# Semaphores in two sets cleared inside the next stage, and the experts' gathered rows in a ring of four

## The reference

```python
mod = jax.nn.silu(c) @ p["w_ada"] + p["b_ada"]          # shifts, scales and gates of both halves
h = rmsnorm(x, p["norm_mix_g"]) * (1.0 + sc1) + sh1
proj = h @ p["w_in"]
qa, fa, ia, ga, bb, cc, vb, mga, mgb = jnp.split(proj, _split_points(), axis=-1)
ya, s_hgrn_new = hgrn2_branch(qa, fa, ia, ga, s_hgrn, lb, p["hgrn_norm_g"])     # gated linear recurrence
yb, s_conv_new = short_conv_branch(bb, cc, vb, s_conv, p["conv_w"], p["conv_b"])
mixed = (jax.nn.sigmoid(mga) * (ya @ p["w_out_hgrn"])
         + jax.nn.sigmoid(mgb) * (yb @ p["w_out_conv"]))
x = x + g1 * (mixed @ p["w_o"])
h2 = (rmsnorm(x, p["norm_ffn_g"]) * (1.0 + sc2) + sh2).reshape(B * T, D)
top_i, top_w = route(h2, p["w_router"], p["router_bias"])      # 8 of 64 experts, from 4 of 8 groups
ffn = (routed_experts(h2, top_i, top_w, p["w_exp_gate"], p["w_exp_up"], p["w_exp_down"])
       + swiglu(h2, p["w_sh_gate"], p["w_sh_up"], p["w_sh_down"]))
x = x + g2 * ffn.reshape(B, T, D)
```

## Time and profile before

| | us |
|---|---|
| median of 3 runs (lowest, highest) | 2221.73 (2220.11, 2222.01) |
| the profiled execution's own time | 2220.11 |
| its span, first to last instruction | 2218.5 |
| TensorE busy, whole span | 1982.7 (89%) |
| expert stage, 1171.3 to 2167.7 | 996.4, TensorE busy 941.9 |
| final stage, 2169.1 to 2218.5 | 49.4, TensorE idle |

### The profile page before, as it was taken

The page is one execution under the profiler, slowest core; times in us unless marked ns, Lnnn a source line. Parts: engine busy times, 40 slices in busy tenths (PEclk is TensorE's granted clock), DMA queues, the critical chain, the costliest instruction groups (busy, mean ns, idle before and its releaser), DMA issues. The chain is left out here.

```text
span 2218.5 us, 32929 instructions
## 1 busy us (share of the span) xinstructions
PE 1982.7 (89%) x9599; PEld 1472.1 (66%) x9601; DVE 1037.9 (47%) x1508; ACT 889.3 (40%) x1213; POOL 346.4 (16%) x321
## 2 busy tenths in 40 slices
PE   4799999799989899797887999999999999999970
PEld 3799999576656566584545767666666776776650
DVE  3210111533327433443625666655555666666656
ACT  4111110234301221211135666656565666666652
POOL 0100100100000000000102222222222232322320
PEclk9899999899989999898988999999999999999995
DMA  6211110111132466334128999999999789879846
GB/s 230 68 47 39 55 40 19 42 42 51 41 92 86 150 220 237 136 135 167 64 94 345 310 299 290 349 340 343 375 343 368 248 264 284 263 237 307 277 98 248
DMA packets 152434, 424.08 MB, mean 191 GB/s; under 512 B 11455, under 2 KB 76211, under 8 KB 127810
## 3 DMA queue, kind: packets, MB, share of 16 engines
q1 hardware_dynamic: 118258, 298.98, 35.8%
q0 software_dynamic: 31488, 114.93, 20.1%
q10 hardware_dynamic: 2640, 9.54, 1.1%
HBM read 345.93 MB, written 77.49 MB: 191 GB/s over the span
## 5 line engine op out<-in xcount | busy, mean ns | idle before, releaser
L1915 DVE TENSOR_TENSOR wexp_lo<-wexp,wexp_hi 128x2048 fp32r<-128x2048 f32 x190 | 426.9, 2289 | 45.8 <-ACT wexp_hi L1867 42.0
L1867 ACT ACTIVATE wexp_hi<-wexp 128x2048 fp32r x190 | 352.8, 1904 | 51.9 <-issue 49.3
L1848 PE MATMUL bank<-wexp_down,hTe 128*128 x736 | 330.6, 592 | 0.0
L1823 PE MATMUL bank<-wexp_hi,x_hi 128*128 128x512 f32 x744 | 300.2, 403 | 4.0 <-DVE wexp_lo L1915 4.0
L1823 PE MATMUL bank<-wexp_hi,x_lo 128*128 128x512 f32 x744 | 291.9, 392 | 0.0
L1823 PE MATMUL bank<-wexp_lo,x_hi 128*128 128x512 f32 x744 | 290.6, 391 | 0.0
L1797 POOL DMA_INDIRECT acc_d<-ob,ixs x92 | 160.0, 1739 | 654.1 <-DMA acc_d<-ob,ixs 280.9
L556 PE MATMUL bank<-hT,wg 128*128 128x344 f32 x768 | 238.0, 464 | 21.1 <-DMA wg<-in_w_in 14.9
L1848 PEld LDWEIGHTS bank<-wexp_down,hTe 128*128 128x128 f32 x736 | 139.1, 189 | 139.4 <-issue 132.3
L556 PEld LDWEIGHTS bank<-hT,wg 128*128 128x128 f32 x768 | 145.2, 194 | 109.6 <-ACT gst L567 15.9
L458 PE MATMUL bank<-hT_hi,w_hi 128*128 128x344 f32 x576 | 186.7, 324 | 14.8 <-DVE w_lo L525 14.8
(11 more groups left out here) (320 smaller groups left out, 2693.5 us busy)
## 6 DMA issues: line engine op xcount, KB each, us to landing
wexp<-in_w_exp_gate SPq DMA_DIRECT2D x64, 1024.0 KB, 7.4
wexp<-in_w_exp_up SPq DMA_DIRECT2D x64, 1024.0 KB, 11.8
wexp_down<-in_w_exp_down SPq DMA_DIRECT2D x64, 1024.0 KB, 11.3
wada<-in_w_ada SPq DMA_DIRECT2D x12, 2048.0 KB, 11.1
w_raw<-in_w_in SPq DMA_DIRECT2D x28, 512.0 KB, 3.9
gates_d<-gst POOLq DMA_DIRECT2D x48, 172.0 KB, 2.1
gate<-gates_d SPq DMA_DIRECT2D x16, 516.0 KB, 5.5
wg<-in_w_in SPq DMA_DIRECT2D x16, 512.0 KB, 4.2
```

The costliest lines, as they stand in the source:

```text
L1823: last = pe.matmul(banks[0][:].rearrange("p (g n) -> p g n", g=2), stat[:, b, k, :], mov[:, b, :, k * FF:(k + 1) * FF], start=(k == 0 and ...
L1848: last = pe.matmul(banks[4 + half][:], hT[:, f, :], wdn[:, bass.ds(slot, 1), f, half * 512:half * 512 + 512].rearrange("p a n -> p (a n)") ...
L1867: act.activation(w_hi[:, b, g, :], wexp[:, bass.ds(e & (RING - 1), 1), g, :].rearrange("p a n -> p (a n)"), ACT.Copy).then_inc(whi_ok, 1)
L1915: dve.tensor_tensor(w_lo[:, b, g, :], wexp[:, bass.ds(e & (RING - 1), 1), g, :].rearrange("p a n -> p (a n)"), w_hi[:, b, g, :], ALU.subtr ...
```

## The change

Two things, in one edit.

Semaphores come from two sets in turn. `next_stage()` no longer opens a block; it gives the names of the set before last free and remembers the last stage's semaphores in `past`. The clears, `tidy(pool)`, stand in POOL's list of the next stage. The last stage has none, so the 20 semaphores of `experts` are not cleared any more.

In the expert stage `xg`, `ix` and `gat` have four buffers, and a block is gathered six blocks ahead of the one that is scattered (AHEAD, 4 before), so POOL's gather in `block_of(i)` is for block i+6 and its buffer is that of block i+2. Blocks 2 and 3 are gathered at once when the stage begins. To make room, `par` and `cT` are placed where they end with the trunk, and the tile of zeros for the pads is 256 instead of 512 wide, read twice by its DMA. DVE waits for the pads before its loop.

```diff
-AHEAD = 4
+AHEAD = 6
...
-        stage = top.enter_context(ExitStack())
-        held = []
+        stages = [top.enter_context(ExitStack()), top.enter_context(ExitStack())]
+        held, past = [], []
...
         def next_stage():
 
-            with nc.Block() as block:
-                @block.gpsimd
-                def _(pool):
-                    for s in held:
-                        pool.sem_clear(s)
+            stages[1].close()
+            stages.reverse()
+            past[:] = held
             held.clear()
-            stage.close()
+
+        def tidy(pool):
+
+            for s in past:
+                pool.sem_clear(s)
...
         @block.gpsimd
         def _(pool):
+            tidy(pool)
 
             with pool.Fori(0, PASSES) as i:
...
                 pool.memset(vblk[:], 0.0).then_inc(const_ok, 1)
+                tidy(pool)
                 pool.sem_inc(gate_read, 1)
...
                 pool.memset(badd[:], 0.0).then_inc(zero_ok, 1)
+                tidy(pool)
...
                     pool.dma_start(xt[0:rows_of(t), t % 2, :], x_rows(t)).then_inc(x_in[t % 2], 16)
+                    if t == 1:
+                        tidy(pool)
...
+                tidy(pool)
                 for r, (f, n) in enumerate(pieces):
...
-            xg = nc.alloc_sbuf_tensor_at("xg", [P, 2, XW], F32, offset=at)
+            xg = nc.alloc_sbuf_tensor_at("xg", [P, RING, XW], F32, offset=at)
...
         def gathered(i, q, ahead):
 
-            return (i - q) * 8 + 16 * ((q + ahead) // 2 + 1)
+            return (i - q) * 4 + 16 * ((q + ahead) // RING + 1)
...
             @block.gpsimd
             def _(pool):
+                for q in range(2, RING):
+                    pool.indirect_dma_start(out=xg[:, q, 0:XW], out_offset=None, in_=xe_d,
+                                            in_offset=bass.IndirectOffsetOnAxis(ap=ix[q][:, 0:1], axis=0)).then_inc(gat[q], 16)
                 pool.memset(none[:], 0.0).then_inc(pad_ok, 1)
...
-                def gather(j, b):
-                    pool.wait_ge(ix_ok, j - 1)
+                tidy(pool)
+
+                def gather(j, q):
+                    pool.wait_ge(ix_ok, j - (RING - 1))
...
-                for j in range(2, 4):
-                    pool.wait_ge(x_tp, j - 1)
-                    pool.wait_ge(wc_ok, j - 1)
-                    gather(j, j % 2)
+                for j in range(RING, AHEAD):
+                    pool.wait_ge(x_tp, j - (RING - 1))
+                    pool.wait_ge(wc_ok, j - (RING - 1))
+                    gather(j, j % RING)
 
                 def block_of(i, q):
                     b = q % 2
                     pool.wait_ge(x_tp, i + 3)
                     pool.wait_ge(wc_ok, i + 3)
-                    gather(i + 4, b)
+                    gather(i + AHEAD, (q + AHEAD) % RING)
                     pool.wait_ge(ob_ok, 2 * i + 4)
...
                 def block_of(i, q):
                     b = q % 2
                     take(i + 2, b)
-                    to_gather(i + 4, b)
+                    to_gather(i + AHEAD, (q + AHEAD) % RING)
...
+                dve.wait_ge(added, 32)
                 blocks(dve, block_of)
```

More of the change, by code:

```diff
@@ L399, in layer @@
             lists = far("lists", [P, ITEMS + AHEAD], U32)
-            ix = [far(f"ix{b}", [P, 1], U32) for b in range(2)]
-            xg = nc.alloc_sbuf_tensor_at("xg", [P, 2, XW], F32, offset=at)
+            ix = [far(f"ix{b}", [P, 1], U32) for b in range(RING)]
+            xg = nc.alloc_sbuf_tensor_at("xg", [P, RING, XW], F32, offset=at)
             next_stage()
@@ L405, in layer @@
             down_in = top.enter_context(nc.semaphore("down_in"))
-            gat = [top.enter_context(nc.semaphore(f"gat{b}")) for b in range(2)]
-            routing(nc, a, sb, sem, banks, ident, hT, xe_d, acc_d, table, starts, total, lists, ix, xg, gat, wexp, wdn,
+            gat = [top.enter_context(nc.semaphore(f"gat{b}")) for b in range(RING)]
+            routing(nc, tidy, a, sb, sem, banks, ident, hT, xe_d, acc_d, table, starts, total, lists, ix, xg, gat, wexp, wdn,
                     up_in, down_in)
@@ L410, in layer @@
             next_stage()
-            experts(nc, a, sb, sem, banks, ident, xe_d, acc_d, table, starts, total, lists, ix, xg, gat, wexp, wdn, up_in,
+            experts(nc, tidy, a, sb, sem, banks, ident, xe_d, acc_d, table, starts, total, lists, ix, xg, gat, wexp, wdn, up_in,
                     down_in)
@@ L1661, in _ @@
                 s.link(dve.tensor_tensor(lists[:, 0:ITEMS], ids[:, 0, :], ids[:, 1, :], ALU.add))
-                for b in range(2):
+                for b in range(RING):
                     dve.tensor_copy(ix[b][:], lists[:, b:b + 1]).then_inc(ix_ok, 1)
@@ L1802, in _, with turn @@
                 pool.wait_ge(added, 16 * n + 32)
-                for b in range(2):
-                    pool.wait_ge(gat[b], 16 * ((n + 5 - b) // 2))
+                for q in range(RING):
+                    pool.wait_ge(gat[q], 16 * ((n + AHEAD + RING - 1 - q) // RING))
             @block.tensor
             def _(pe):
-                def turn(j, b, here):
-                    pe.wait_ge(gat[b], here)
+                def turn(j, q, here):
+                    pe.wait_ge(gat[q], here)
                     if j is not 0:
@@ L1813, in turn @@
                     for k in range(KD):
-                        last = pe.transpose(banks[1 + k // 4][:, (k % 4) * P:(k % 4 + 1) * P], xg[:, b, k * P:(k + 1) * P],
+                        last = pe.transpose(banks[1 + k // 4][:, (k % 4) * P:(k % 4 + 1) * P], xg[:, q, k * P:(k + 1) * P],
                                             ident[:])
@@ L1839, in block_of @@
                     last.then_inc(h_tp, 1)
-                    turn(i + 2, b, gathered(i, q, 2))
+                    turn(i + 2, (q + 2) % RING, gathered(i, q, 2))
                     up(i + 1, 1 - b)
@@ L1931, in _ @@
                 take(0, 0)
-                to_gather(2, 0)
+                to_gather(4, 0)
                 rest_of_weights(e, 0, 0)
@@ L1940, in _ @@
                 e = entry(dve, 2, 1, E - 1)
-                weight(e, 2, 32)
+                weight(e, 2, 16)
                 rest_of_weights(e, 2, 0)
```

49 lines of the change are left out of this document (25 added, 24 removed).

## The result

The changed kernel takes 2195.89 us (median of 4 runs, 2195.29 to 2197.40) against 2221.87 us before (4 runs, 2220.11 to 2222.97): a ratio of 0.9887, 95% interval 0.9873 to 0.9901. That is 26.0 us less. The forecast was 2193 us in 2174 to 2210. On another chip, later, the same pair gave 2196.04 and 2221.13 us, ratio 0.9886 (0.9870 to 0.9901). The profiled execution took 2195.8 us (2220.11 before), its span is 2194.0 us. The profiled execution before was the shortest of its four, so the two spans differ by 24.5 us where the medians differ by 26.0.

The account below looks back on a forecast made before the run. It took expert-stage scatters, each waiting for the last one's landing, to bound the kernel, TensorE's pace hardly shorter. 13.4 + 15 = 28.4 us off 2220.1 gave 2191.7; with the median 1.6 us higher, 2193, range 2174 to 2210.

Parts of the forecast that it names:

- The clearing blocks: Seven blocks between stages that only clear semaphores: 177 clears and seven barriers leave the path, 13.4 us, bounds 11.5 to 14.5.
- The start of the expert stage: Two gathers moved to the front and DVE's new wait for the pads: 0 to 4 us, value 0.
- The ring: Four gather buffers in the expert stage: of 35.6 us TensorE loses, 19.2 stay; gain 16.4, valued at 15 us.
- the chain: Expert-stage scatters, each waiting for the one before to land: 948.3 us, 29 of it air; it stays after the change.
- The lag it allows: How late a scatter may be before TensorE loses time: 5.9 us before, 12.7 after, 6.8 gained once per slow stretch.
- the long stretch: 30 scatters from 1399.75 to 1716.31: 316.6 us against TensorE's 290.6; of 26.0 too much, 6.8 absorbed, 19.2 stay.
- The 1.4 us for longer landings: Allowance for scatter landings growing 0.05 us over 29 links, as the same bytes must move in less time.
- What was to show it: Signs named beforehand, including 70 or more scatters 0.8 us after a landing and TensorE's expert-stage loss near 20 us.
- A: Rival: in the expert stage scatters land faster and all 35.6 us come back; 49 us gained, 2173 us; 17%.
- B: Rival: full DMA engines hold TensorE to their pace, the expert stage gains nothing; 13.4 us gained, 2208 us; 17%.
- C: Rival: expert-stage scatters land later as weight loads overlap them more often; 2252 us at 0.8 us more per landing; 7%.
- D: Rival: the clears do not leave the path, because a POOL queue is waited for; 15 us gained only, 2207 us; 4%.

Follow-up runs that it names:

- e1_clears: The kernel before with only the clears moved into the next stage on POOL, the ring of gathered rows left two deep: 2204.82 us, ratio 0.9927.
- e5_thin: The changed kernel with only an eighth of each weight transfer of experts 4 and up: 2174.73 us, ratio 0.9788.
- e3_two: The changed kernel with scatters going to two accumulators in turn, the second added in the last stage by accumulating transfers: 2189.88 us, ratio 0.9861.
- e7_extra: The changed kernel with one more 0.52 MB transfer per block on POOL's queue: 2237.12 us, ratio 1.0070.

## Why the prediction was right

**The clearing blocks: 13.4 us forecast, 13.8 measured.** The clears' spacing and the seven barriers gave it. That POOL's work in the stages behind hides them holds too: in e1_clears no stage that took clears in is more than 0.2 us longer. In the mixers the first gate product starts at 411.39 us, when its weights land, where it was 412.55.

**The start of the expert stage: 0 forecast.** From the release to the third turn it took 19.3 us, 20.0 before. Nothing came back here.

**The ring: 15 us forecast, 13.1 measured (35.6 to 22.5).** The mechanism was right in each part. The named wait went, the chain stayed (316.56 and 316.72 us for the same 30 scatters), and the next limit is the landing that the index copy waits for. The lag it allows was forecast as 5.9 and 12.7 us; measured plateaus are 7.9 and 15.3. The sums took turns 10.02 us apart, but at the plateau TensorE goes at the chain's 10.92 us: two such intervals make the first 7.7, three make the second 15.4. The difference, which is what counts, is 7.4 against 6.8.

The term mis-sized is how much of this lag the long stretch gets. I gave it all 6.8 us. But the deeper ring also lets the lag of the blocks ahead be carried in: the first scatter of the stretch stands 1388.98 - 1379.80 = 9.2 us behind its turn (5.9 before), the last one 15.0. So 5.8 us were absorbed and TensorE lost 310.9 - 290.6 = 20.3 us over these turns, not 19.2, and another 2.2 us in the two intervals behind, while the lag ran off. That is 22.5. The 1.4 us for longer landings was an error: landings did not grow, the stretch is unchanged to 0.2 us. That it brought the value from 16.4 to 15, nearer to the 13.1 measured, is luck. All of the loss lies between the turns at 1430 and 1713 us.

Where the 13.1 us came from is worth seeing. Over the long stretch and the two intervals behind it the kernel before lost 25.0 us, so the deeper ring saved 2.5 there. The other 10.6 us were lost outside of it, in short runs of slow scatters, and there all of it came back.

**The sum.** 13.8 + 12.3 us in place of 13.4 + 15, and about 1.5 us given back by the other stages. Such shifts show between all of these programs (see the first turns in the table) and have no term in the prediction; they are within its range.

**What was to show it.** No clears between two barriers, no gather ahead of TensorE's transposes, 81 scatters (70 or more were named) released by a landing, the loss ahead of the hh transposes and inside the long stretch: all as written. The mean landing could not be read, since the trace of the changed kernel doesn't pair its scatters with their landings; that the same 30 scatters take the same time stands for it. The whole chain gives a bound, as an estimate: 935.2 us for 91 intervals, less the 0.8 us between a landing and the next start, is at most 9.5 us for the mean landing, where 9.27 was measured before.

**The rivals.** A (all comes back) needed landings that the ring doesn't shorten; e5_thin shows the 2174.7 us it forecast as 2173, but only with the weights thinned. The Trainium skill's "DMA: Bandwidth & Descriptors", section "Anatomy of one DMA", by which the chain would never bind, does not hold for these scatters: the chain binds until the weights' traffic is cut, and even then the shortest landing is 6.0 us against the 3.2 estimated from it. B (full DMA engines hold TensorE) was wrong in its reason: e3_two keeps TensorE busy at a share of 1.01, for all but 3.8 us of waits for weights. C did not occur, but its arithmetic is real: e7_extra, whose scatters land later for another reason, ends slower than before. D is excluded by e1_clears. The Trainium skill's section "Queues, rings and completion order" of "DMA: Bandwidth & Descriptors", which has engines take queues in turn by the packet, speaks against a slowdown by backlog alone; here scatters got faster when the weights' bytes were cut. These runs don't tell turn-taking at full engines from a backlog.

## What to carry to other kernels

When an engine that issues transfers waits in line for one of them, the profile names the transfer queued behind it. Follow one block back to the first wait that isn't explained by another, and sum that chain by itself before pricing the fix: a buffer absorbs lag once per slow stretch, less what the blocks ahead have already put in, and the chain's own surplus stays. To gain more, cut the chain (here into two), and price at the same time what the cut has to put together again.

## What was not expected of the hardware

- POOL's add of 128x1024 float32 took 2.33 to 3.31 us, and VectorE's operations of the same shape beside it took 3.2 to 3.5 us in place of 1.2 to 1.3. Taking work off VectorE this way cost more than it saved.
- A full share of the DMA engines was not a fixed rate: 411 GB/s with loads alone in the last stage, 332 to 369 in the rows of the experts, 295 with accumulating transfers and stores, all at a share of 1.00 to 1.06.
- POOL's drain at the end of the expert stage, 10.6 us after the start of its last scatter, takes 5.37 us (4.64 before); it lies on the path to the last stage:

```profile
L1733 POOLq DRAIN  x1: 5372/5372/5372, 2138.6 to 2138.6; - x1
```

- One clear takes 44 ns inside the stages and took 38 in blocks of its own.
